# Seven places for the experts' weights instead of six, three of them filled during the output projection, x1 kept in DRAM, and the last sum without Pool

## What is computed

```python
m_lat = merge_branches(...)            # ends in: (gated sum of both branches) @ w_out
h_lat = h_lat + gt1 * rmsnorm(m_lat, norm_gains[l, 1])        # this is x1 in the kernel
f_lat = hier_moe(modulate(rmsnorm(h_lat, norm_gains[l, 2]), sh2, sc2), *moe_params)
h_lat = h_lat + gt2 * rmsnorm(f_lat, norm_gains[l, 3])        # the output

def hier_moe(u, ...):     # 4 groups of 8 experts; top-1 group, top-2 experts in it
    ...
    for e in range(N_EXPERTS):                                # 32 experts
        h = jax.nn.silu(flat @ w_gate[e]) * (flat @ w_up[e])  # 1024 -> 256
        y = y + gates[:, e:e + 1] * (h @ w_down[e])           # 256 -> 1024
```

## Time and profile before

| | us |
|---|---|
| median of three runs | 1671.73 (1669.41 to 1672.78) |
| the profiled execution | 1671.29 |
| its span, first to last instruction | 1669.0 |

### The profile page before, as it was taken

How to read it: one execution, slowest core, us unless ns; L and a number is a source line. 1 busy time by engine, 2 the same in 40 slices (tenths; PEclk the granted TensorE clock), 3 DMA queues, 4 the chain that set the end, 5 groups by cost and what they waited for, 6 DMA issues and landing times. The chain is left out here.

```text
span 1669.0 us, 37651 instructions
## 1 busy us (share of the span) xinstructions
PE 1368.8 (82%) x16476; PEld 826.2 (50%) x16476; DVE 653.5 (39%) x1000; ACT 580.8 (35%) x876; POOL 244.4 (15%) x194
## 2 busy tenths in 40 slices
PE   5799999991998899999996879999998357776780
PEld 3455545550888888888884324344444322222220
DVE  1436676765444444454541540533333500000004
ACT  3235554543555555555551741000011011111112
POOL 0011111220311333333310000000000001001004
PEclk9999999996899999999998989999999578898895
DMA  8205445535433222332206029553230849999974
GB/s 346 82 23 155 126 143 144 164 87 137 100 81 89 69 66 79 85 86 79 80 16 233 1 92 387 201 189 139 101 130 25 340 176 394 404 416 407 398 298 176
DMA packets 163608, 281.41 MB, mean 169 GB/s; under 512 B 42739, under 2 KB 141171, under 8 KB 153475
## 3 DMA queue, kind: packets, MB, share of 16 engines
q1 hardware_dynamic: 157508, 249.81, 42.5%
q0 software_dynamic: 5952, 29.36, 4.5%
HBM read 234.05 MB, written 53.49 MB: 172 GB/s over the span
## 5 line engine op out<-in xcount | busy, mean ns | idle before, releaser
L1797 PE MATMUL ex_pgu<-ex_w,hT 128*32 128x512 f32 x1024 | 135.7, 690 | 62.2 <-DMA ex_w<-in_w_experts 60.9
L389 PE MATMUL pr_ps<-hT,pr_w 128*128 128x512 f32 x384 | 173.4, 609 | 15.3 <-ACT pr_rate L450 10.8
L389 PEld LDWEIGHTS pr_ps<-hT,pr_w 128*128 128x128 f32 x384 | 74.0, 195 | 110.2 <-issue 89.9
L940 DVE COPY_PREDICATED rc_T<-masks_sb,rc_ps 128x512 f32<-128x512 uint32 x96 | 65.2, 729 | 158.1 <-PE rc_ps L736 158.1
L1797 PEld LDWEIGHTS ex_pgu<-ex_w,hT 128*32 128x32 f32 x1024 | 39.4, 124 | 147.9 <-issue 145.9
L1207 PE MATMUL mg_ps<-hT,mg_w 128*128 128x512 f32 x256 | 111.2, 592 | 1.0 <-PEq L1101 1.0
L1663 DVE TENSOR_TENSOR ex_sig<-ex_sig,ex_pgu 128x256 f32<-128x256 f32 x16 | 6.7, 421 | 215.0 <-ACT ex_sig L1657 215.0
L702 PE MATMUL rc_ps<-rc_KR,rc_BK 64*128 64x128 f32 (+1 forms) x768 | 55.7, 292 | 37.4 <-DMA rc_KR<-kr_chunks 36.2
L736 PE MATMUL rc_ps<-rc_T,rc_Z 64*64 64x64 f32 x3840 | 74.7, 222 | 11.7 <-issue 10.4
L1207 PEld LDWEIGHTS mg_ps<-hT,mg_w 128*128 128x128 f32 x256 | 48.6, 190 | 62.6 <-issue 62.6
L862 ACT ACTIVATE rc_Z<-rc_ps 128x1024 f32<-128x1024 f32 (+1 forms) x48 | 41.5, 881 | 102.8 <-PE rc_ps L702 102.8
(11 more groups left out here) (304 smaller groups left out, 2409.1 us busy)
## 6 DMA issues: line engine op xcount, KB each, us to landing
ex_w<-in_w_experts SPq DMA_DIRECT2D x32, 3072.0 KB, 18.5
bonus_sb<-in_ada_w SPq DMA_DIRECT2D x16, 1024.0 KB, 7.2
mg_w<-in_w_merge SPq DMA_DIRECT2D x8, 1792.0 KB, 7.7
pr_w<-in_w_prep SPq DMA_DIRECT2D x8, 1664.0 KB, 6.6
kr_chunks<-pr_KR SPq DMA_DIRECT2D x16, 768.0 KB, 4.8
bk_chunks<-pr_BK SPq DMA_DIRECT2D x16, 768.0 KB, 6.8
rc_BK<-bk_chunks SPq DMA_DIRECT2D x24, 512.0 KB, 5.3
rc_KR<-kr_chunks SPq DMA_DIRECT2D x24, 512.0 KB, 5.3
```

The lines of the kernel that those rows point to most:

```text
L389: last = pe.matmul(lat_bank[:, :], wv[:, j * KT + kt, :], hT[:, kt, lat], start=(kt == 0), stop=(kt == KT - 1))
L940: dve.copy_predicated(T[u][:, d, :, :, :].rearrange("p q b t -> p b q t"), level(int(s[1:]), d), by_side).then_inc(dve_s, 1)
L1797: last = pe.matmul(p_gu[v][rows, :], xT[:, v, k, rows], up(u)[:, k, :], start=(k == 0), stop=(k == KT - 1))
```

## The change

- `WSLOTS` is 7, and the places are pairs of a region for gate and up weights and a region for down weights, in buffers that other stages leave: place 0 in `bonus` and the end of `hT`, 1 in `ry` and `py`, 2 in `w_merge`, 3 in the space of `w_out` (free after the output projection), 4 and 5 in new space, `merged` and `pl_u`, 6 in new space and in masks that are no longer read (the masks are reordered so that the three that are lie in front).
- Every expert is loaded by two DMAs, 2 MiB and 1 MiB.
- Experts 0 to 2 (`EARLY`) are loaded by SP in `project_out`, after the loads of `x`; experts 3 to 5 at the start of `route`. In `experts`, expert n = 6 is loaded without a wait for `down`, and n >= 7 waits for `down` of the pair whose place it takes, `(n - 7) // 2`.
- `x1` is stored to DRAM tile by tile in `project_out`, and loaded again (2 MiB, one DMA) after pair 13. The gathered rows and their turned form, and temporaries of `route`, take its room in `hT`.
- In the last sum DVE adds `x1` for all tiles; POOL adds nothing.
- ACT runs a Sqrt on one column before the last copy of `y`.

```diff
-WSLOTS = 6
+WSLOTS, EARLY = 7, 3
@@ project_out, sync
                 for t in range(NT):
                     sp.dma_start(x1[:, t, :], I["x"][t * P:t * P + P, :]).then_inc(xload, 16)
+                for u in range(EARLY):
+                    load_expert(sp, I, ew[u], wl[u], u * P * EXPERT_W)
                 for t in range(NT):
+                    sp.wait_ge(dve_x, t + 1)
+                    sp.dma_start(g["x1_dram"][t * P:t * P + P, :], x1[:, t, :]).then_inc(x1st, 16)
                     sp.wait_ge(dve_f, t + 1)
                     sp.dma_start(g["f_dram"][t * P:t * P + P, :], f[:, t % 2, :]).then_inc(fst[t % 2], 16)
                 for u in range(2):
                     sp.wait_ge(fst[u], NT // 2 * 16)
+                sp.wait_ge(x1st, NT * 16)
@@ route, sync
-                for u in range(WSLOTS):
-                    load_expert(sp, I, w, wl, u, u * P * EXPERT_W)
+                for u in range(EARLY, FIXED):
+                    load_expert(sp, I, ew[u], wl[u], u * P * EXPERT_W)
@@
-def load_expert(sp, I, w, wl, u, at):
-    sp.dma_start(w[:, u, :], flat(I["w_experts"], at, P * EXPERT_W).rearrange("(p n) -> p n", p=P)).then_inc(wl[u], 16)
+def load_expert(sp, I, place, sem_, at):
+    up, dn = place
+    n = KT * 2 * FE
+    src = flat(I["w_experts"], at, P * EXPERT_W).rearrange("(p n) -> p n", p=P)
+    sp.dma_start(up, src[:, 0:n]).then_inc(sem_, 16)
+    sp.dma_start(dn, src[:, n:EXPERT_W]).then_inc(sem_, 16)
@@ experts, sync
-                for p in range(FIXED // 2, PAIRS):
-                    r = p - FIXED // 2
-                    sp.wait_ge(s["down"], r + 1)
-                    for place, rank in zip(places(p), (r, NE - FIXED - 1 - r)):
-                        e = sp.value_load(R["order"][0:1, rank:rank + 1], min_val=0, max_val=NE - 1)
-                        load_expert(sp, I, w, wl, place, sp.snap(e * NWE))
+                for n in range(FIXED, NE):
+                    r = n // 2 - FIXED // 2
+                    rank = NE - FIXED - 1 - r if n % 2 else r
+                    if n >= WSLOTS:
+                        sp.wait_ge(s["down"], (n - WSLOTS) // 2 + 1)
+                    e = sp.value_load(R["order"][0:1, rank:rank + 1], min_val=0, max_val=NE - 1)
+                    load_expert(sp, I, ew[n % WSLOTS], wl[n % WSLOTS], sp.snap(e * NWE))
                 sp.wait_ge(s["down"], PAIRS - 2)
                 sp.dma_start(gt, g["mod_rows"][:, 3 * D:4 * D].to_broadcast([P, D])).then_inc(vec_loaded, 16)
                 sp.dma_start(gain, I["gains"][2:3, :].to_broadcast([P, D])).then_inc(vec_loaded, 16)
+                sp.dma_start(x1, g["x1_dram"].rearrange("(t p) n -> p t n", p=P)).then_inc(vec_loaded, 16)
@@ experts, sync, the stores of the output
-                    if t + 1 < NT:
-                        sp.wait_ge(out_s, t + 1)
-                    else:
-                        sp.wait_ge(normed_s, NT + 1)
+                    sp.wait_ge(out_s, t + 1)
@@ experts, gpsimd
-                for t in range(NT - 1):
-                    pool.wait_ge(normed_s, t + 1)
-                    pool.tensor_tensor(acc[:, t, :], acc[:, t, :], x1[:, t, :], ALU.add).then_inc(out_s, 1)
@@ experts, scalar
+                    if p + 1 == PAIRS:
+
+                        act.activation(st[:, 0, 3:4], g["small"][:, 1:2], ACT.Sqrt)
                     act.wait_ge(s["down"], p + 1)
@@ experts, vector
-                dve.wait_ge(vec_loaded, 32)
+                dve.wait_ge(vec_loaded, 48)
-                    dve.scalar_tensor_tensor(out=acc[:, t, :], in0=acc[:, t, :], scalar=st[:, t, 2:3], in1=gt, op0=ALU.mult, op1=ALU.mult).then_inc(normed_s, 1)
-                dve.drain()
-                dve.tensor_tensor(acc[:, NT - 1, :], acc[:, NT - 1, :], x1[:, NT - 1, :], ALU.add).then_inc(normed_s, 1)
+                    dve.scalar_tensor_tensor(out=acc[:, t, :], in0=acc[:, t, :], scalar=st[:, t, 2:3], in1=gt, op0=ALU.mult, op1=ALU.mult)
+                    dve.drain()
+                    dve.tensor_tensor(acc[:, t, :], acc[:, t, :], x1[:, t, :], ALU.add).then_inc(out_s, 1)
```

More of the change, by code:

```diff
@@ L40 @@
 LEVELS = (2, 4, 8, 16)
-MASKS = ["ident", "heads", "eye", "before", "ones", "both", "both_back"]
+LATE_MASKS = ["ident", "before", "ones"]
+MASKS = LATE_MASKS + ["heads", "eye", "both", "both_back"]
 MASKS += [x for b in (1, 2, 4, 8, 16, "32t") for x in (f"level{b}", f"level{b}_back")]
@@ L1258, in _, with project_out @@
                 add_bias(KT - 1, ps[0][0])
-def project_out(nc, g, I, merged, x1, logits, w, w_loaded):
+def project_out(nc, g, I, merged, x1, logits, w, w_loaded, ew, wl):
     NT = SEQ // P
@@ L1390, with route @@
 TILES = PAIRS + SPILL
-WSLOTS = 6
+WSLOTS, EARLY = 7, 3
 EXPERT_W = KT * 2 * FE + 2 * D
-def route(nc, g, I, logits, R, w, wl):
+def route(nc, g, I, logits, R, ew, wl):
     NT, NR = SEQ // P, NE - FIXED
@@ L1406, in route @@
         sel, te, oh1, oh2, msk = t8("rt_sel"), t8("rt_te"), t8("rt_oh1"), t8("rt_oh2"), t8("rt_msk")
-        O1, O2, both, pre, tmp = (t32(f"rt_x{j}") for j in range(5))
+        O1, O2, both, pre, tmp = (late[:, j * NT * NE:(j + 1) * NT * NE].rearrange("p (t e) -> p t e", e=NE) for j in range(5))
         ma, mb, e2, w1 = (sb(f"rt_m{j}", [P, NT, 1]) for j in "abcd")
@@ L1588, in _, with experts @@
                 dve.tensor_copy(R["spill_tiles"][:, :], incl[:, NE - 1:NE])
-def expert_weights(nc, ctx):
-    w = ctx.enter_context(nc.sbuf_tensor("ex_w", [P, WSLOTS, EXPERT_W], F32))
-    return w, [ctx.enter_context(nc.semaphore(f"ex_w{u}")) for u in range(WSLOTS)]
-def load_expert(sp, I, w, wl, u, at):
-    sp.dma_start(w[:, u, :], flat(I["w_experts"], at, P * EXPERT_W).rearrange("(p n) -> p n", p=P)).then_inc(wl[u], 16)
-def experts(nc, g, I, R, w, wl, x1, out):
+def load_expert(sp, I, place, sem_, at):
[4 more added lines that the diff above has]
+    sp.dma_start(dn, src[:, n:EXPERT_W]).then_inc(sem_, 16)
+def experts(nc, g, I, R, ew, wl, small, out):
     NT = SEQ // P
@@ L1619, in experts @@
         NWE, NYE = P * EXPERT_W, P * D
[L1620 to L1628, removed]
+        up = lambda u: ew[u][0].rearrange("p (k n) -> p k n", k=KT)
+        dn = lambda u: ew[u][1].rearrange("p (k n) -> p k n", k=2)
+        got = [[small["top"][:, (2 * t + j) * D:(2 * t + j + 1) * D] for j in range(2)] for t in range(NT)]
+        sq = small["top"][:, 2 * NT * D:(2 * NT + 1) * D]
+        x1, acc = (ew[u][0].rearrange("p (t n) -> p t n", t=NT) for u in (5, 1))
+        gt, gain = (ew[5][1][:, q * D:(q + 1) * D] for q in range(2))
+        y_spill = got[0][0]
         st = sb("cb_st", [P, NT, 4])
@@ L1698, in experts @@
         vec_loaded, gath, combined = sem("cb_loaded"), [sem(f"cb_g{t}") for t in range(NT)], sem("cb_stored")
-        scaled_s, acc_s, root_s, normed_s, out_s = (sem(f"cb_{n}") for n in ("scaled", "acc", "root", "normed", "out"))
+        scaled_s, acc_s, root_s, out_s = (sem(f"cb_{n}") for n in ("scaled", "acc", "root", "out"))
         with nc.Block() as block:
@@ L1874, in scale @@
                     act.wait_ge(gath[t], 32)
-                    act.activation(got[:, t, 0, :], got[:, t, 0, :], ACT.Copy, scale=R["gate"][:, 0, t:t + 1]).then_inc(scaled_s, 1)
+                    act.activation(got[t][0], got[t][0], ACT.Copy, scale=R["gate"][:, 0, t:t + 1]).then_inc(scaled_s, 1)
                 def root(t):
@@ L2040, in program @@
             merge(nc, g, I, py, ry, merged, w_merge, merge_loaded, load_out)
-            project_out(nc, g, I, merged, x1, logits, w_out, w_out_loaded)
-        R = {"slot": sb("slot", [P, 2, SEQ // P], U32), "gate": sb("gate", [P, 2, SEQ // P]), "tok": sb("tok", [P, TILES], U32),
-             "order": sb("order", [P, NE - FIXED], I32),
-             "spill_expert": sb("spill_expert", [P, SPILL], I32), "spill_tiles": sb("spill_tiles", [P, 1], I32)}
-        with ExitStack() as inner:
-            w, wl = expert_weights(nc, inner)
-            route(nc, g, I, logits, R, w, wl)
-            g["gathered"] = [inner.enter_context(nc.semaphore(f"ex_gathered{v}")) for v in range(2)]
-            experts(nc, g, I, R, w, wl, x1, out)
+            line = lambda t: t[:, :, :].rearrange("p a b -> p (a b)")
+            NU, ND = KT * 2 * FE, 2 * D
+            spare, left = w_merge[:, :, :, :].rearrange("p u m n -> p (u m n)"), pb["space"][:, :]
+            ew = [(line(g["bonus"]), line(g["hT"])[:, SEQ * KT:]), (line(ry), line(py)), (spare[:, 0:NU], spare[:, NU:NU + ND]), (left[:, 0:NU], left[:, NU:NU + ND])]
+            wl = [mixers.enter_context(nc.semaphore(f"ex_w{u}")) for u in range(WSLOTS)]
+            project_out(nc, g, I, merged, x1, logits, w_out, w_out_loaded, ew, wl)
+            top = msb("ex_top", [P, 2 * NU + ND])
+            ew += [(top[:, NU:2 * NU], top[:, 2 * NU:]), (line(merged), line(pb["u"])), (top[:, 0:NU], line(g["masks"])[:, len(LATE_MASKS) * P:])]
+            small = {"y": left[:, NU + ND:], "sig": spare[:, NU + ND:NU + ND + 2 * FE], "h": spare[:, NU + ND + 2 * FE:], "hT": line(pb["pw"]), "top": top}
```

(6 more changed lines are left out.)

34 lines of the change are left out of this document (17 added, 17 removed).

## The result

The changed kernel takes 1653.53 us (median of four, 1651.96 to 1654.97), the kernel before beside it 1672.26 us. The ratio is 0.9887, 95% interval 0.9867 to 0.9908: 18.7 us or 1.1% less. Predicted were 1652 us and a range of 1647 to 1661. The profiled execution took 1651.96 us, its span is 1649.8 us.

The account below looks back on a forecast made before the run. The weight stream after down(0) was taken as the bound. From the profiled 1671.29 us: -7.3 (gather) - 7.6 (one load fewer) - 2.5 (deeper queue) + 0.8 (split) - 2.7 (last sum) = -19.3, so 1652 us; range 1647 to 1661.

Parts of the forecast that it names:

- The bound and its place: Experts' stage: from 1377 us on, the bytes still to come and the start of their stream, behind down(0), set the end.
- Loads in the output projection, 0: Output projection: loading experts there gains 0 by itself and costs 0, between 0 and +4 us.
- R, the first gather: Start of the experts' stage: with an emptier queue the gather lands sooner and down(0) ends 7.3 us earlier (4.8 to 8.7).
- Rival 1: First gather: expert 6's packets get ahead of it, so it gains 0 to 2 us; 1658 to 1659 us; chance 0.13.
- One load fewer: Weight stream behind down(0): 25 expert loads instead of 26, a gain of 7.6 us (7.2 to 9.1).
- a deeper queue: Weight stream: one more expert in flight when a down ends fills empty time, a gain of 2.5 us (0 to 4.4).
- the split: Weight stream: two DMAs for each expert, with smaller packets, cost 0.8 us, at most 4 us.
- The last sum, 2.7 us: Last sum: additions without POOL and an earlier table load gain 2.7 to 2.8 us (1.4 to 3).
- the step with the table load: Last sum: moved before the last copy of y, the 1.28 us load is covered; first root at 1649.3 instead of 1650.6.
- Rival 2: Output projection: x lands with the early weights near 1252 instead of 1230, about 16 us lost; about 1668 us; chance 0.06.
- Rival 3: Stream after down(0): each of 25 additional DMAs has an unhidden cost, 2.2 us making +55; about 1707 us; chance 0.04.
- Rivals 4 and 5: Seventh place fails, only gather and last sum gain, about 1661 us, chance 0.05; all bounds good, 1645 to 1648, 0.10.

Follow-up runs that it names:

- six_places: The changed kernel with six places instead of seven, x1 and the last sum's two rows in place 2 instead of 5: 1671.22 us, ratio 0.999 to the kernel before.
- early_none: The changed kernel with no expert loaded in the output projection (EARLY = 0): 1654.93 us, ratio 0.9884 to the kernel before.
- split_before: The kernel before with each expert loaded by two DMAs, 2 MiB and 1 MiB, into the same six places: 1676.22 us, ratio 1.003.
- hold_six: The changed kernel, but SP waits for the first gather to land before issuing expert 6: 1650.67 us, ratio 0.9857 to the kernel before.
- tail_before: The kernel before with the last sum's additions on DVE for all four tiles instead of POOL for three: 1672.25 us, ratio 0.9996.
- root_late: The changed kernel with the early Sqrt behind ACT's empty loop over extra tiles, not before the last copy of y: 1651.05 us, ratio 0.9866 to the kernel before.

## Why the prediction was right

The time lay in the range and 1.5 us from the point, and the sum met its own execution: 1652.0 predicted, 1651.96 measured. That it came so close is luck. Three terms were wrong by more than a microsecond and cancelled: the start of the stage brought 3.4 us and not 7.3, the stream 16.4 and not 9.3, the last sum 1.5 and not 2.7, and the clock behind the last wait took back 1.7 that stood in no term.

**The bound and its place: right.** The end is set by the stream of weights behind `down(0)`. `six_places` shows it most plainly: with the same early loads, a quick gather and the shorter last sum, but six places, the time is that of the kernel before. The last `gate_up` started at 1596.1, where 1598.5 was forecast.

**Loads in the output projection, 0: right** that they hold up nothing in the end (logits at 1302.2 instead of 1301.8, though the first `f` reaches PE 2.1 us later, of which 0.7 is the stage's later start) and that by themselves they bring little: `early_none` costs 2.1 us up to the first `y`, and its time can't be told from the changed kernel's.

**R, the first gather: wrong.** 7.3 us (4.8 to 8.7) were predicted, 3.4 measured from the end of routing, and of these `split_before` has 1.4 with no early load at all (38.8 against 40.2), so the early loads have 2.0. The step that failed is when expert 6's packets begin, and what they then do to the gather. I let them begin 3.1 us after the gather's issue, 0.9 us for SP and 2.2 us from the issue to the first packet, when most of the gather would be through. SP issued 0.2 us after POOL. And the 2.2 us were misread: the view of the earlier trace rows begins at 1304, behind the first packets. The rate in 1302 to 1306 us of the trace before, in slices of 0.1 us:

```profile
GB/s 0 0 0 0 0 0 0 0 0 0 0 0 0 1475 1475 492 0 0 246 0 0 0 0 0 0 0 0 492 1229 737 983 246 0 246 0 0 492 737 983 983
```

The loads are issued from 1302.36 on and the first packets are there at 1303.3, 0.9 us later, as for expert 6 in the changed kernel (1338.47 and 1339.4). So they began 1.1 us after the gather's issue and ahead of its own packets. The bound failed too: sharing packet by packet was to cost 8.7 us at most, and the gather took 10.3, because its packets began 3 us late and then had to share: in 1343 to 1345 us of the changed kernel its queue had 20% of the engines' time and expert 6's had 78%. Rival 1 named this and gave it R of 0 to 2 (by its own sum 1657 to 1659 us, not 1658 to 1659). `hold_six` shows the missing 4.9 us where the prediction had put them.

**One load fewer, a deeper queue and the split, together 9.3 us: too small.** 16.4 were measured (238.6 to 222.2). The term that was mis-sized is depth. I bounded it by the empty time, 4.4 us (2.1% of 220 us are 4.6), as if more depth could only fill holes. With 7.6 us for one load, depth less split brought 8.8 us and not 1.7. The split was too small as well: 0.8 us predicted, at most 4; with six places it costs 3.3 to 4.6. `six_places` against `hold_six` changes the number of places: 22.5 us in the stream, of which 7.6 is one load; 14.9 us are depth when the loads are split. The rate accounts for it: at 395 instead of 425 GB/s 222 us would be 17 us longer, an estimate from the two rows above. Open is why `six_places` is 2.8 us slower in the stream than `split_before`.

**The last sum, 2.7 us: the step with the table load failed.** 1.5 were measured, near the bound of 1.4 that stood for this case. DVE's part is as predicted (`tail_before` alone has 1.7). I checked that ACT had time for the moved load and not that the table would still be there behind the loop; `root_late` recovers the rest.

**Rivals.** Rival 1 came true in its mechanism and not in its time, since the depth made up for it. Rival 2 didn't come: the median of the loads of `x` is 10.9 us from issue to landing, 11.5 before. Rival 3 is refuted at its price of 2.2 us for each DMA (which rests on the misread row), though a cost of 0.13 to 0.18 us is there with six places. Rivals 4 and 5 didn't come. The Trainium skill (DMA: Bandwidth & Descriptors, Anatomy of one DMA) fits its 2.0 us for each DMA on DMAs issued from GpSimd, and these are SP's. As a price in a full queue it isn't borne out: 26 more DMAs cost 3.3 to 4.6 us in `split_before`, where the estimate by the page is 52. The Trainium skill (ScalarE: Activation LUTs, What ACT_TABLE_LOAD costs) gives 2.66 us for a switch of tables; taking the load off the chain brought 1.1 to 1.5 us, so here too 1.28 is the better number.

## What to carry to other kernels

Where DMAs set the end, count the bytes that are in flight at the moment when the next load is issued. A place more can be worth three times its bytes (22.5 us for a load of 7.6), and the empty slices of the profile are no upper bound for it. Before a delay is read from a view, the view has to begin ahead of the issue. What is latency-critical at the start of a stage (a small gather that everything waits for) wants the queues to itself: hold the large load until it has landed, if there is room later. And a table that is brought in ahead has to be brought in behind the last loop that could change it.

## What the runs showed of the hardware that I had not expected

A gather of 128 rows of 4 KiB is at PE 4.4 to 4.6 us after its issue when no weights move (six traces) and 10.3 us after it beside one expert's 16 and 8 KiB packets, though it was issued 0.2 us ahead of them: its first packet came after 4.7 us instead of 1.7. In the stream, 1400 to 1580 us, the median from issue to landing of a gather is 22.3 us beside packets of 24 KiB and 14.7 us in `split_before`, where only the size of the weights' packets differs. So the small transfers gained here when the large ones beside them came in smaller packets, and the large ones paid: 406 to 397 GB/s. And the last `gate_up` and `down` took 15.4 or 17.1 us by the granted clock alone.
